# Finishing prompt rows inside the expert loop of a routed decoder step, in place of a pass over all rows behind it

## What is computed

```
h2  = modulate(rmsnorm(x2, norm2_g), sh2, sc2)
g   = top-1 of 4 groups; e1, e2 = top-2 of the 4 experts in g
out = sum over e in (e1, e2) of gate_e * (silu(h2 @ w_gate[e]) * (h2 @ w_up[e])) @ w_down[e]
x3  = x2 + g2 * out
y   = rmsnorm(x3, final_norm_g)        # y_prompt (2048 rows), y_sample (64 rows)
```

## Time and profile before

| | us |
|---|---|
| median of 3 runs | 1169.64 (1169.25 to 1170.22) |
| the profiled execution, its own time | 1168.66 |
| its span, first to last instruction | 1166.9 |
| first `out` of the expert loop starts | 730.5 |
| last scatter (tile 39) is issued | 1104.8 |
| last PE product (sample rows) ends | 1144.9 |

### The profile page before, as it was taken

How to read it: one execution, slowest core, us unless ns; L and a number is a source line. 1 busy time by engine, 2 the same in 40 slices (tenths; PEclk the granted TensorE clock), 3 DMA queues, 4 the chain that set the end, 5 groups by cost and what they waited for, 6 DMA issues and landing times. The chain is left out here.

```text
span 1166.9 us, 18010 instructions
## 1 busy us (share of the span) xinstructions
PE 1075.8 (92%) x5413; PEld 807.6 (69%) x5414; DVE 776.5 (67%) x1274; ACT 509.0 (44%) x715; POOL 308.4 (26%) x359
## 2 busy tenths in 40 slices
PE   3799999999969989999999989999999999999992
PEld 2357777776546667777787646888888788888860
DVE  4557475747789973369887778555777555555375
ACT  5133242522132325446665344555565445455273
POOL 0046262625041000030000003333333433333344
PEclk9799999999889999999999999999999999999997
DMA  9933646467776449485766566797789777775597
GB/s 280 316 108 101 193 137 193 150 180 226 200 190 164 136 160 242 167 234 201 252 218 222 176 221 229 244 292 221 220 257 291 216 216 216 218 216 110 111 358 310
DMA packets 166412, 244.75 MB, mean 210 GB/s; under 512 B 65783, under 2 KB 123271, under 8 KB 162207
## 3 DMA queue, kind: packets, MB, share of 16 engines
q1 hardware_dynamic: 138001, 171.05, 45.8%
q0 software_dynamic: 16112, 54.88, 18.0%
q10 hardware_dynamic: 12246, 18.14, 4.6%
HBM read 169.36 MB, written 75.84 MB: 210 GB/s over the span
## 5 line engine op out<-in xcount | busy, mean ns | idle before, releaser
L126 PE MATMUL experts_psGU<-weights_we_hi,experts_x_hi 128*128 (+1 forms) x344 | 140.6, 409 | 2.0 <-DVE experts_x_lo L2667 1.0
L127 PE MATMUL experts_psGU<-weights_we_hi,experts_x_lo 128*128 (+1 forms) x344 | 136.1, 395 | 0.0
L128 PE MATMUL experts_psGU<-weights_we_lo,experts_x_hi 128*128 (+1 forms) x344 | 136.0, 395 | 0.0
L2493 POOL DMA_INDIRECT acc_d<-experts_o_sb,experts_to_col x40 | 71.2, 1779 | 209.1 <-DMA acc_d<-experts_o_sb,experts_to_col 99.9
L126 PE MATMUL front_psM<-front_hT_hi,front_w_hi 128*128 128x512 f32 x256 | 106.7, 417 | 0.9 <-DVE front_hT_lo L1005 0.7
L2686 DVE TENSOR_TENSOR experts_o_sb<-experts_psD,experts_g2r 128x1024 f32<-128x1024 f32 x43 | 52.7, 1225 | 74.5 <-PE experts_psD L128 74.5
L127 PE MATMUL front_psM<-front_hT_hi,front_w_lo 128*128 128x512 f32 x256 | 101.6, 397 | 0.0
L128 PE MATMUL front_psM<-front_hT_lo,front_w_hi 128*128 128x512 f32 x256 | 101.2, 395 | 0.0
L126 PEld LDWEIGHTS experts_psGU<-weights_we_hi,experts_x_hi 128*128 128x128 f32 x344 | 64.7, 188 | 19.9 <-issue 5.2
L128 PEld LDWEIGHTS experts_psGU<-weights_we_lo,experts_x_hi 128*128 128x128 f32 x344 | 64.7, 188 | 15.6
L2657 DVE TENSOR_TENSOR weights_we_lo<-weights_we_raw,weights_we_hi (+1 forms) x64 | 75.4, 1219 | 0.0
(11 more groups left out here) (521 smaller groups left out, 2521.0 us busy)
## 6 DMA issues: line engine op xcount, KB each, us to landing
front_raw<-in_w_ada SPq DMA_DIRECT2D x24, 1024.0 KB, 7.8
weights_we_raw<-in_exp_w_gate SPq DMA_DIRECT2D x16, 1024.0 KB
weights_we_raw<-in_exp_w_up SPq DMA_DIRECT2D x16, 1024.0 KB
weights_wd_raw<-in_exp_w_down SPq DMA_DIRECT2D x16, 1024.0 KB
front_xraw<-in_x_prompt SPq DMA_DIRECT2D x4, 2048.0 KB, 10.9
part_d<-middle_ev ACTq DMA_DIRECT2D x16, 512.0 KB, 3.0
middle_xt<-in_x_prompt SPq DMA_DIRECT2D x16, 512.0 KB, 4.9
middle_part<-part_d SPq DMA_DIRECT2D x16, 512.0 KB, 5.5
```

The source lines that it names most:

```text
L126: pe.matmul(out, l_hi, r_hi, start=start, stop=False)
L127: pe.matmul(out, l_lo, r_hi, start=False, stop=False)
L128: return pe.matmul(out, l_hi, r_lo, start=False, stop=stop)
L2493: pool.indirect_dma_start(acc_d, bass.IndirectOffsetOnAxis(tc[:, u, :], 0), osb[:, u, :], None, compute_op=ALU.add).then_inc(added, 16)
```

## The change

The rows of a token's later slot are finished inside the loop.

- Routing marks which of a token's two slots comes later in the tile order: POOL gives that slot's gate a minus sign (9 small operations, `signs`), and DVE reads the sign back as `R.last` and takes the absolute value of the gate (two small operations).
- POOL builds a table `R.rows` with four index columns for each tile: rows of h2 to fetch; rows of acc_d to add onto (earlier slots, and samples); rows of acc_d to fetch (later slots); rows of y_prompt to store (later slots). Rows that a column doesn't mean carry an index out of bounds and are skipped.
- `scatter` becomes `sums`: the indexed add onto acc_d for the earlier slots, and behind it an indexed fetch from acc_d that adds onto osb for the later slots.
- Two tiles later in the order, ACT squares osb with a row sum (`row_squares`), POOL adds eps and raises to -0.5 (`power`), DVE makes one refining step in three 128x1 operations and scales the row into a new buffer `fo` (`row_norm`), and POOL stores it to y_prompt (`store`). In iteration s all this is for tile s-3. DVE's `row_norm(s-3)` stands ahead of `out(s-1)`, which writes the same buffer.
- g2r has one buffer in place of two; the sample rows' gate row g2s is loaded late.
- The eight loads, the 16 stores, their squares, roots and norms, the flags and the six small products behind the loop are gone. The three late tiles and the samples are finished as before.

```diff
+        self.nil = k.sb(st, "nil", [1, 6])
+        self.acc_in, self.y_out = [[k.sem(f"f_{n}{u}") for u in range(2)] for n in ("acc_in", "y_out")]
...
+        pool.tensor_copy(self.cols[:, u, :], R.rows[:, bass.ds(t, 1), :].rearrange("p a n -> p (a n)")).then_inc(self.ic_ok, 1)
...
...
+            for n, done in enumerate(W.acc_in + 2 * W.y_out):
+                pool.dma_start(W.nil[:, n:n + 1], a["norm2_g"][0:1, n:n + 1]).then_inc(done, 16)
+            pool.wait_ge(mx, 2)
+            up, down = sgn[:, 0, :], sgn[:, 1, :]
+            pool.tensor_tensor(up, km2[:, 0, :], km2[:, 1, :], ALU.subtract).then_inc(signs, 1)
...
+            pool.tensor_scalar(down, down, 1.0, None, ALU.subtract).then_inc(signs, 1)
...
+            for i, x in enumerate((up, down)):
+                pool.tensor_tensor(gt[:, :, i], gt[:, :, i], x, ALU.mult).then_inc(signs, 1)
...
+            dve.sem_inc(gates_ok, 1)
...
                    .broadcast_to([P, n, 2, NCOL]), ALU.is_equal)
+                if j == 0:
+                    dve.wait_ge(signs, 9)
                 gated = dve.tensor_tensor(A[:, 1, r], A[:, 0, r], b2(gt[:], NCOL), ALU.mult)
...
             cp(R.gate[:], psS[:, NCOL:2 * NCOL])
+            ts(R.last[:], R.gate[:], 0.0, None, ALU.is_lt)
+            ch.link(dve.scalar_tensor_tensor(out=R.gate[:], in0=R.gate[:], scalar=-1.0, in1=R.gate[:], op0=ALU.mult, op1=ALU.max))
...
+            sp.wait_ge(W.wlo, 4 * (NE - 1))
+            sp.dma_start(g2s[:], mod_d[1:ROWS, 5 * D:6 * D].unsqueeze(1).broadcast_to([NSEQ, LSEQ, D])).then_inc(s_in, 16)
             last = last_tile(sp)
-            sp.wait_ge(bulk_go, 1)
-            for g in range(ROW_PAIRS):
-                if g in FREE:
-                    sp.wait_ge(*FREE[g])
-                if g == ROW_PAIRS // 2:
-                    sp.wait_ge(gu_mm, last + 1)
-                sp.dma_start(rows[g][:], pair(acc_d[0:TP, :], g)).then_inc(px_in[g], 16)
-                if g == ROW_PAIRS // 2 + 1:
-                    sp.wait_ge(d_mm, last)
-                    sp.dma_start(xs[:], acc_d[TP:TOK, :]).then_inc(s_in, 16)
-                    sp.dma_start(x2[:], x2s_d[:, :]).then_inc(s_in, 16)
+            sp.wait_ge(samples_go, 1)
+            sp.wait_ge(d_mm, last)
+            sp.dma_start(xs[:], acc_d[TP:TOK, :]).then_inc(s_in, 16)
+            sp.dma_start(x2[:], x2s_d[:, :]).then_inc(s_in, 16)
...
         def expert_pool(pool):
             last = last_tile(pool)
+            pool.memset(osb[:], 0.0).then_inc(osb_ok, 1)
...
+            pool.wait_ge(osb_ok, 2)
+            pool.wait_ge(rows_ok, 8)
             pool.sem_inc(freed, FREED0)
-            pool.memset(eps[:], EPS).then_inc(eps_ok, 1)
...
+            def sums(t, u):
...
                 pool.wait_ge(oev, OEV0 + t + 1)
+                pool.sem_inc(fence, 1)
                 if not isinstance(t, int) or t:
                     pool.wait_ge(added, 16 * t)
                     pool.sem_inc(freed, 1)
                 pool.sem_inc(fence, 1)
-                pool.indirect_dma_start(acc_d, bass.IndirectOffsetOnAxis(tc[:, u, :], 0), osb[:, u, :], None,
-                                        compute_op=ALU.add).then_inc(added, 16)
+                pool.indirect_dma_start(acc_d, bass.IndirectOffsetOnAxis(W.cols[:, u, 1:2], 0), osb[:, u, :], None,
+                                        bounds_check=TOK - 1, oob_is_err=False, compute_op=ALU.add).then_inc(added, 16)
+                pool.indirect_dma_start(osb[:, u, :], None, acc_d, bass.IndirectOffsetOnAxis(W.cols[:, u, 2:3], 0),
+                                        bounds_check=TP - 1, oob_is_err=False, compute_op=ALU.add).then_inc(acc_in[u], 16)
+            def power(t, u):
+                pool.wait_ge(fsq, FSQ0 + t + 3)
+                pool.sem_inc(fence, 1)
+                pool.tensor_scalar(fss[:, u, 1:2], fss[:, u, 0:1], EPS, None, ALU.add).then_inc(powers, 1)
+                pool.wait_ge(powers, 2 * t + 5)
+                pool.tensor_tensor(fss[:, u, 2:3], fss[:, u, 1:2], half[:], ALU.pow).then_inc(powers, 1)
+            def store(t, u, to):
+                pool.wait_ge(normed, NORM0 + t + 3)
+                pool.sem_inc(fence, 1)
+                pool.indirect_dma_start(y_p, bass.IndirectOffsetOnAxis(to, 0), fo[:, u, :], None,
+                                        bounds_check=TP - 1, oob_is_err=False).then_inc(y_out[u], 16)
             for t in range(2, 6):
                 pool.wait_ge(xt_ps, t - 1)
                 W.gather(pool, R, h2_d, t, t % 2)
                 if t >= 4:
-                    scatter(t - 4, t % 2)
+                    power(t - 6, t % 2)
+                    sums(t - 4, t % 2)
             with pool.Fori(6, last + 1, 2) as t:
                 for d in range(2):
                     pool.wait_ge(xt_ps, t + d - 1)
+                    pool.sem_inc(fence, 1)
+                    pool.wait_ge(acc_in[d], 8 * (t + d - 6) - 8 * d + 16 + ACC0)
+                    pool.sem_inc(fence, 1)
+                    pool.wait_ge(y_out[d], 8 * (t + d - 6) - 8 * d + YOUT0)
+                    pool.sem_inc(fence, 1)
                     W.gather(pool, R, h2_d, t + d, d)
-                    scatter(t + d - 4, d)
+                    power(t + d - 6, d)
+                    sums(t + d - 4, d)
+                    store(t + d - 6, d, W.cols[:, d, 3:4])
             end = end_tile(pool)
             pool.tensor_copy(tcf[:], R.to[:, bass.ds(end, LATE)]).then_inc(late_ok, 1)
+            pool.tensor_copy(last_to[:], R.rows[:, bass.ds(end + 4, 2), 3:4]).then_inc(late_ok, 1)
...
                                         ).then_inc(late_in[d], 16)
+            power(end - 2, 0)
+            store(end - 2, 0, last_to[:, 0, :])
             pool.wait_ge(late_in[0], 16)
             pool.wait_ge(oev, OEV0 + end + 1)
             pool.tensor_tensor(fix[:, 0, :], fix[:, 0, :], osb[:, 0, :], ALU.add).then_inc(own_sum, 1)
-            pool.wait_ge(store_ok, 1)
+            power(end - 1, 1)
...
-            for n in ORDER[:-1]:
-                if n < ROW_PAIRS:
-                    pool.wait_ge(pair_done, DONE[n])
-                    for r in range(2):
-                        pool.indirect_dma_start(y_p, bass.IndirectOffsetOnAxis(store_to[:, 2 * n + r:2 * n + r + 1], 0),
-                                                rows[n][:, r, :], None, bounds_check=TP - 1, oob_is_err=False
-                                                ).then_inc(py_out[n], 16)
...
+            for d in range(LATE):
+                pool.wait_ge(late_done, d + 1)
+                to = keep_to[:, d:d + 1] if d < LATE - 1 else tcf[:, d:d + 1]
+                pool.indirect_dma_start(y_p, bass.IndirectOffsetOnAxis(to, 0), fix[:, d, :], None,
+                                        bounds_check=TP - 1, oob_is_err=False).then_inc(late_out, 16)
...
+            def gate_rows(t):
+                act.wait_ge(oev, OEV0 + t)
...
+            def row_squares(t, u):
+                act.wait_ge(acc_in[u], 8 * t - 8 * u + 16 + ACC0)
+                act.wait_ge(fsq, FSQ0 + t + 2)
+                act.wait_ge(normed, NORM0 + t + 1)
+                act.activation(junk[:], osb[:, u, :], ACT.Square, scale=1.0 / 32, accum_out=fss[:, u, 0:1]).then_inc(fsq, 1)
...
                     x_hi_of(s + 1, 1 - u)
+                    row_squares(s - 3, 1 - u)
                     silu(s, u)
-                    gate_rows(s - 1, 1 - u)
+                    gate_rows(s - 1)
...
...
-                dve.tensor_tensor(osb[:, u, :] if to is None else to, psD[:], g2r[:, u, :], ALU.mult).then_inc(oev, 1)
+                if to is None:
+                    dve.wait_ge(normed, NORM0 + t + 1)
+                dve.tensor_tensor(osb[:, u, :] if to is None else to, psD[:], g2r[:], ALU.mult).then_inc(oev, 1)
...
+            def row_norm(t, u):
...
+                dve.wait_ge(powers, 2 * t + 6)
+                dve.scalar_tensor_tensor(out=w, in0=y0, scalar=y0, in1=v, op0=ALU.mult, op1=ALU.mult).then_inc(fstep, 1)
...
+                dve.tensor_scalar(h, w, -0.5, 1.5, ALU.mult, ALU.add).then_inc(fstep, 1)
+                dve.wait_ge(fstep, STEPS * t + 2 * STEPS + 2)
+                dve.tensor_tensor(y, y0, h, ALU.mult).then_inc(fstep, 1)
+                dve.wait_ge(fstep, STEPS * t + 2 * STEPS + 3)
+                dve.wait_ge(y_out[u], 8 * t - 8 * u + YOUT0)
+                dve.scalar_tensor_tensor(out=fo[:, u, :], in0=osb[:, u, :], scalar=y, in1=F.gn[:],
+                                         op0=ALU.mult, op1=ALU.mult).then_inc(normed, 1)
...
                     x_lo_of(s + 1, 1 - u)
                     hidden(s, u)
+                    row_norm(s - 3, 1 - u)
                     out(s - 1, 1 - u)
...
             out(end, 0)
-            late_parts()
             with dve.If((code & 1) > 0):
...
-            late_flags()
             hidden(end + 2, 0)
+            row_norm(end - 1, 1)
             kept_rows()
             out(end + 1, 1)
             hidden_lo(end + 2)
-            store_rows()
```

(10 more changed lines are left out.)

227 lines of the change are left out of this document (104 added, 123 removed).

## The result

The changed kernel takes 1323.45 us (median, 1322.74 to 1323.85) where the kernel before takes 1169.93 beside it (1169.25 to 1170.32): a ratio of 1.131, 95% interval 1.129 to 1.132. It is slower by 13%, not by the 8% that were forecast, and the time lies above the range's upper end of 1312 us. The direction and the place were right, the size was not.

What follows compares the result with a forecast made beforehand. PE bounds the loop at 9.54 us a tile, transfers the part behind; the change adds a chain of waits. 98 + 3.5 + 0.4 + 3.1 - 11 = +94 on 1168.66 us gives 1262 us, range 1188 to 1312.

Steps and rivals of the forecast that it cites:

- the circle: In the loop, waits from out through POOL and row_norm to the next out: 12.2 us a tile, 2.66 over 9.54.
- One of its signs: In the loop's profile after, POOL would have no idle time over 1.1 us between its steps.
- the second term: In the loop's chain, POOL's add onto acc_d is issued in 1.61 us, the scatter's median.
- A rule against a row: Paragraph on the loop: the scatter at 884.97 took 1.61 us beside a DVE split, so the contention rule was disagreed with.
- rival 1: In the loop, skipped rows make add, fetch and store cheaper to issue: chain 9.8 to 11.0, 1174 to 1218 us; chance 0.11.
- 2 (cheaper issues): In the loop, the chain falls below 9.5 us, PE sets the pace and all is hidden: 1158 us; chance 0.10.
- 3 (POOL held by DVE): In the loop, POOL waits out DVE's splits, 2.4 us in 28 or so tiles: +67 us, 1329 us; chance 0.05.
- 4 (clock): In the loop, PE's clock falls; at 1.2 GHz throughout over 1500 us; chance 0.03, with a chain over 13.3 us.
- 5: Whole kernel: the change moves nothing, or chain and gain cancel, within 0.2%; chance 0.03.
- Head: Start to out(2): +3.9 us; POOL's operations at the loop's start delay gather(2) by 2 us, covered by that tile's distance.
- Tail: Out(39) to the end: -7.9 us; 12 us in place of 22 behind PE's end, out(39) to out(41) 22.1, +3.1.
- The first case: In the loop, the chain holds with full-cost issues: 1218 to 1303 us, likeliest 1262; chance 0.68.

Runs made afterwards that it cites:

- experiment 3: The changed kernel with POOL's store ahead of the sums in its iteration: 1273.7 us.
- experiment 4: The changed kernel with POOL's power ahead of index copy and gather, and the store ahead of the sums: 1202.3 us.
- experiment 1: The kernel before with four more semaphore increments on POOL ahead of the scatter, to start it some 0.2 us later: 1176.0 us (before 1170.4).
- experiment 2: The changed kernel without DVE's splits of weights inside the loop: 1278.4 us.
- experiment 7: The changed kernel with early squares, power between add and fetch, early gather(2), and splits waiting for a semaphore raised ahead of the add: 1197.3 us, ratio 1.020.
- Experiment 12: The changed kernel with gather(2) issued ahead of POOL's list of tables at the loop's start: 1318.4 us, ratio 1.126.
- experiment 8: The changed kernel with ACT copying the finished row to fo, row_norm behind out and splits, POOL reordered, gather(2) early: 1197.5 us, ratio 1.024.
- experiment 9: As experiment 8, but DVE's row_norm, now of tile s-4, stands behind hidden_lo: 1178.5 us, ratio 1.007.

## Why the prediction was right or wrong, point by point

**What bounds the kernel, and the circle: right.** Every link of the chain and its order came as told. The forecast of `row_norm` waiting for POOL and of PE idling ahead of down is in the rows above, and experiments 3 and 4 take links out and get their price back. One of its signs was wrong: POOL was to have no idle time over 1.1 us between its steps, but it idles 4.55 us ahead of each add. That follows from the chain itself, whose part on DVE and whose way to the add (1.93 + 1.26 + 1.04 us) POOL spends waiting.

**The size of the links.** From the rows at 884.86 to 898.33, against the prediction's terms:

| link | forecast | measured |
|---|---|---|
| end of out to start of add | 1.04 | 1.14 |
| add | 1.61 | 1.64, 2.65 or 3.70; mean 2.69 |
| gap and adding fetch | 1.91 | 0.31 + 1.61 = 1.92 |
| gap and store | 1.28 | 0.31 + 1.04 = 1.35 |
| index copy | 0.76 | 0.20 |
| wait and gather | 1.77 | 0.83 + 1.00 = 1.83 |
| power with its waits | 0.62 | 0.96 (the power itself 0.57, not 0.25) |
| DVE's small operations and scaling | 1.93 | 2.05 |
| gap and out | 1.26 | 1.37 |
| sum | 12.2 | 10.8 + add |

The guess for the adding fetch was exact, that for the power was 0.3 us too small, and the index copy was 0.56 us too dear. All links together give 12.44 with an undisturbed add, 0.24 above the forecast: 9 us over 37 steps.

The index copy's row tells more than its size. The copy of 0.62 us was read at 886.72, 0.14 us behind the scatter's end and inside the `wd_lo` of 884.98 to 887.30, and it ended at 887.34, 0.04 us behind that split. In the kernel before, all 18 copies that start behind the scatter and inside a split end 0.04 to 0.05 us behind the split. Where no DVE instruction runs beside it, the same copy takes 0.18 us:

```profile
1059.09 0.18 POOL L2022 COPY weights_idx_col<-all_idx 128x1 int32 x1
```

(Copies that start 0.57 us before the scatter ahead of them has ended take 0.77 us, but this one starts behind it.) So the prediction put the mark of DVE's hold on POOL into its sum as the price of a copy.

**The step that failed** is the second term, "the add is issued in 1.61 us", and with it the paragraph "A rule against a row". It costs 42 of the 60 us between forecast and result. The row at 884.97 was taken as proof that splits leave no mark on a scatter. It was an alignment in which the mark doesn't show: the scatter started only 0.08 us ahead of the end of one split, and 1.53 us from that end to its own is what it needs anyway; the next split began 0.01 us behind it and didn't count. The rows held counterexamples. The scatter's maximum is 3676 ns. The scatter of 2.40 us at 876.88 stood only in the bound of 13.4 us, without a cause. The copy of 0.62 us is a third. And the store of 1.66 us at 1153.76, which was held against rival 1, started inside DVE's scaling of 1153.30 to 1154.58 and ended 0.84 us behind it. The changed kernel's add starts 0.10 us later behind `out`, and this tenth moves it into the split. In the kernel before, the one scatter that began inside a `wd_lo`, and the split:

```profile
904.08 3.68 POOL L2493 DMA_INDIRECT acc_d<-experts_o_sb,experts_to_col  x1 [3.58 <-DMA acc_d<-experts_o_sb,experts_to_col]
```

```profile
903.99 2.28 DVE L2663 TENSOR_TENSOR weights_wd_lo<-weights_wd_raw,weights_wd_hi  x1
```

3.68 us, ending 1.49 us after the split. The Trainium skill, GPSIMD Engine Reference, Key points, says that GpSimd shares its SBUF interfaces with VectorE and contends with DVE instructions that have two SBUF inputs. The trace and experiments 1, 2 and 7 agree with it, and add what that passage doesn't say: the wait is for the instruction in progress at the start, and is not repeated for later ones.

**Rivals.** 1 and 2 (cheaper issues): wrong. The skipped rows cost POOL the full issue: add 1.64, fetch 1.61, store 1.04 us. 3 (POOL held by DVE): its mechanism is half of the truth. It expected 2.4 us in 28 tiles on add and fetch, 1329 us; measured are 1.0 or 2.06 us in 27 adds and none on the fetch. That its 1329 us lie so near the measured 1323 is luck: the hold came to 42 us, not 67, and other links and the head made up for it. 4 (clock): the granted clock did fall, from 1.00 (2.4 GHz) to 0.89 in the mean of the stretch, with PE idle 3.70 us ahead of one down and 1.92 ahead of another, but it cost nothing, since each step but the one of 15.45 us is the add's duration plus 10.8 us whatever the clock. 5: no.

```profile
888.95 0.50 PE L126 MATMUL experts_psD<-weights_wd_hi,experts_hT_hi 128*128 x1 [3.70 <-DVE experts_hT_lo L2726]
...
902.19 0.49 PE L126 MATMUL experts_psD<-weights_wd_hi,experts_hT_hi 128*128 x1 [1.92 <-DVE weights_wd_lo L2710]
```

**Head: too small by 7 us.** "Which that tile's distance covers" was wrong: gather(2) was issued at 719.60 and PE's transposes waited 2.89 us for its landing. Experiment 12 prices the list at 5 to 6 us. The rest, 1 to 2 us, can't be told from what the head varies by from trace to trace: the kernel before has its first `out` at 730.5, and experiment 1, with the same head, at 733.2.

```profile
716.04 2.40 POOL L2501 TENSOR_SCALAR all_rows<-all_far 128x48 int32<-128x48 int32 x2
...
719.60 2.43 POOL L2027 DMA_INDIRECT weights_xg<-h_d,weights_idx_cols  x1 [0.81 <-POOL weights_idx_cols L2024]
```

```profile
729.38 0.96 PE L2858 MATMUL experts_psX<-all_ident,weights_xg 128*128 128x128 f32 x5 [2.89 <-DMA weights_xg<-h_d,weights_idx_cols]
```

**Tail: right in sum, by luck.** From the last product of PE (1311.97) to the end it was 8.9 us, where 12 had been taken and 22.0 stood before: 3 us better. Out(39) to out(41) took 25.5 us, where 22.1 had been taken: 3 us worse. Two errors of one size cancel.

**Chances and range.** The first case held 0.68 with an upper end of 13.3 us a step. A rule that named this very pair of instructions got 0.05 on the strength of one row. Given the 3676 ns that stood unexplained in the same rows, it should have had several times that, and the range an end of 1330.

## What to carry to other kernels

Work moved into a loop with room on every engine can still lengthen it: write down which step waits for which from one use of a buffer to the next, and sum that circle; here it cost 150 us where the pass it replaced gave back 13. Before one row is held against a rule, look at every row of that line and explain its longest: a start time that happens to fall between two instructions proves nothing. And what is saved should be looked for on the circle first: moving one 1.35 us store ahead of another step gave back 50 us, while the same amount of work stayed on POOL.

## What the runs showed of the hardware

- **POOL waits out a DVE instruction with two SBUF inputs that is in progress when POOL starts.** An adding transfer then ends 1.5 us after the instruction, a plain gather 0.9 to 1.0 us after it, a 128x1 addition 0.09 us after it (2.16 us in place of 0.24), an index copy 0.04 us after it. From the expert loop's start on, in the 14 traces of this case, 391 adding transfers start inside a split or the scaling of `row_norm`; all end 1.45 us or more after it but five, which start within 0.03 us of the DVE instruction's own start and aren't held. Of the 643 that start beside no such instruction none takes over 1.69 us. DVE instructions that start later, be it by 0.03 us, don't hold it, nor does `x_lo`, which has one input in PSUM.
- **The hold seems to go the other way too.** In experiment 8 DVE's three comparisons of 128x64 took 3.53 us while POOL ran a sum of 128x1024 with two SBUF inputs (2.36 us from 1153.60), and 0.57 us in experiment 9, where no such sum ran beside them. No experiment was made on it alone.

```profile
1152.49 3.53 DVE L2797 TENSOR_SCALAR experts_sample_row<-experts_sample_f,experts_to_late_f 128x64 f32<-128x64 f32 x3
```

```profile
1136.01 0.57 DVE L2800 TENSOR_SCALAR experts_sample_row<-experts_sample_f,experts_to_late_f 128x64 f32<-128x64 f32 x3
```

- **An indexed transfer with half of its rows skipped is issued in the same time as a full one:** 1.64 us with an addition (1.61 full), 1.04 plain (0.96 to 1.00 full), 0.31 us between two of them.
